# The first projection of a two-block transformer kernel: operands split before the squares, and the gates' arithmetic moved back

## What is computed

```python
def _layer(x, norm_w, w_in, qk_gain_q, qk_gain_k, rpb, conv_w, a_log, dt_bias, dn_norm_w, w_out):
    h = _rmsnorm(x, norm_w)                       # x * rsqrt(mean(x*x) + EPS) * norm_w
    proj = jnp.einsum('bld,de->ble', h, w_in)
    aq, ak, av, az, dq, dk, dv, dz, b_f, a_f, b_b, a_b = _split_proj(proj)
    aq = _rmsnorm(heads(aq, NA_HEADS), qk_gain_q)
    ak = _rmsnorm(heads(ak, NA_HEADS), qk_gain_k)
    attn = _neighbourhood_attention(aq, ak, heads(av, NA_HEADS), rpb) * jax.nn.silu(az)
    qkv = jax.nn.silu(_centred_depthwise_conv(jnp.concatenate([dq, dk, dv], axis=-1), conv_w))
    dq, dk, dv = jnp.split(qkv, 3, axis=-1)
    dq, dk, dv = _l2norm(to_bhld(dq)), _l2norm(to_bhld(dk)), to_bhld(dv)
    # gates: beta = sigmoid(b), g = -exp(a_log) * softplus(a + dt_bias)
    ...
    return x + y
```

## Time and profile before

| | |
|---|---|
| median of 3 runs | 2832.3 us (2832.14 to 2832.37) |
| the profiled execution | 2832.62 us, span of the core 2830.8 us |
| mean granted TensorE clock | 0.977 of full |
| PE busy | 2679.3 us, 95% of the span |
| PEld / DVE / ACT / POOL busy | 76% / 41% / 38% / 44% |
| span 0 to 10 us | PE busy 0.00 us |
| span 10 to 20 / 20 to 30 / 30 to 40 us | PE busy 3.24 / 4.87 / 7.36 us |
| span 40 to 50 us | PE busy 10.00 us |
| first projection, PE's matmuls | 16.1 us to 434.2 us of the span |

### The profile page before, as it was taken

The page is one execution under the profiler, slowest core; times in us unless marked ns, Lnnn a source line. Parts: engine busy times, 40 slices in busy tenths (PEclk is TensorE's granted clock), DMA queues, the critical chain, the costliest instruction groups (busy, mean ns, idle before and its releaser), DMA issues.

```text
span 2830.8 us, 33041 instructions
## 1 busy us (share of the span) xinstructions
PE 2679.3 (95%) x13337; PEld 2150.5 (76%) x13337; DVE 1174.1 (41%) x1631; ACT 1072.3 (38%) x1593; POOL 1243.0 (44%) x717
## 2 busy tenths in 40 slices
PE   6999998988969999999999999899999999999997
PEld 4778875667858888887888777666788888788885
DVE  6465666655663222222222327667532222222223
ACT  4443445634544422233322333656443222232222
POOL 2222222554026555556555554311455454565554
PEclk8999998989989999999999999999999999999998
DMA  3222415441143222223222232100222222323331
GB/s 132 90 88 96 150 45 203 135 142 52 38 145 115 97 97 97 97 97 104 97 97 97 98 130 91 40 8 1 99 95 98 97 97 97 112 90 108 116 103 69
DMA packets 93880, 273.20 MB, mean 97 GB/s; under 512 B 25944, under 2 KB 26136, under 8 KB 93600
## 3 DMA queue, kind: packets, MB, share of 16 engines
q1 hardware_dynamic: 93728, 271.09, 28.2%
HBM read 240.05 MB, written 31.00 MB: 96 GB/s over the span
## 4 chain that ended last, share of the span: by engine, by line
PE 82%; DVE 6%; POOL 5%; ACT 3%; DMA 2%; issue 1%; SPq 1%; POOLq 0%; DVEq 0%; ACTq 0%
PE ps L350 23%; PE ps L351 23%; PE ps L352 23%; PE ps L875 2%; ACT t L366 2%; PE ps L895 2%; PE ps L859 2%; POOL t L1336 1%; POOL t L1333 1%; PE ps L491 1%; DVE t L1009 1%; PE ps L1437 1%; POOL t L1834 1%; POOL t L415 1%; ACT t L958 1%
## 5 line engine op out<-in xcount | busy, mean ns | idle before, releaser
L366 ACT ACTIVATE t<-t 128x1024 fp32r<-128x1024 f32 (+5 forms) x961 | 735.3, 810 | 1392.1 <-PE ps L352 650.6
L415 POOL TENSOR_TENSOR t<-t 128x1024 fp32r<-128x1024 f32 x356 | 862.5, 2427 | 874.7 <-ACT t L366 874.6
L350 PE MATMUL ps<-t 128*128 128x512 f32 (+1 forms) x3034 | 1199.0, 395 | 47.5 <-DVE t L528 18.4
L352 PE MATMUL ps<-t 128*128 128x512 f32 (+1 forms) x3034 | 1181.4, 389 | 0.0
L351 PE MATMUL ps<-t 128*128 128x512 f32 (+1 forms) x3034 | 1181.3, 389 | 0.0
L350 PEld LDWEIGHTS ps<-t 128*128 128x128 f32 x3034 | 572.0, 189 | 184.8 <-issue 53.0
L351 PEld LDWEIGHTS ps<-t 128*128 128x128 f32 x3034 | 572.5, 189 | 120.7 <-issue 6.5
L352 PEld LDWEIGHTS ps<-t 128*128 128x128 f32 x3034 | 571.9, 188 | 118.5
L2050 DVE SCALAR_TENSOR_TENSOR t<-ps,t 128x512 f32<-128x512 f32 x192 | 132.7, 691 | 315.0 <-PE ps L352 277.2
L2106 POOL TENSOR_TENSOR t<-t 128x512 fp32r<-128x512 f32 x84 | 108.7, 1295 | 332.4 <-ACT t L366 332.4
L2027 DVE TENSOR_TENSOR t<-ps,t 128x512 f32<-128x512 f32 x84 | 58.1, 692 | 396.2 <-PE ps L352 396.2
(11 more groups left out here) (167 smaller groups left out, 1884.6 us busy)
## 6 DMA issues: line engine op xcount, KB each, us to landing
t<-in_wts_dram SPq DMA_DIRECT2D x356, 512.0 KB, 3.5
t<-pj SPq DMA_DIRECT2D x39, 512.0 KB, 5.9
pj<-t SPq DMA_DIRECT2D x32, 512.0 KB, 2.7
t<-in_rpb_dram SPq DMA_DIRECT2D x8, 736.0 KB, 7.7
t<-in_xT_dram SPq DMA_DIRECT2D x8, 512.0 KB, 10.5
t<-grow_d SPq DMA_DIRECT2D x8, 512.0 KB, 8.4
t<-beta_d SPq DMA_DIRECT2D x8, 512.0 KB, 9.5
t<-in_xT_dram SPq DMA_DIRECT2D x16, 256.0 KB, 4.0
```

Of the source, the lines that this page charges most:

```text
L350: e.matmul(out, ah, bh, start=start, stop=False)
L352: return e.matmul(out, al, bh, start=False, stop=stop)
L366: return e.activation(out, in_, fn, scale=scale)
L415: e.tensor_tensor(lo[:], T.raw[n % NR][:], hi[:].bitcast(F), SUB).then_inc(*w_lo.up(n))
```

## The change

- **Operands first.** ACT makes H of all eight chunks, then splits weights 1 and 2, then makes the eight squares; before, H and square alternated, behind the weights 0 to 2. DVE makes all eight Lo, then adds all seven squares; POOL adds none. The squares now take turns in t1 and t3.
- **x first.** SP issues weights 0, then the eight chunks of x, then weights 1 to 5.
- **Tile 0 by chunks.** PE runs both halves of chunk k before chunk k + 1. The sum for the factor is behind tile 1 instead of in the middle of tile 0.
- **Order of tiles.** The first eight behind the gates are silu, dv, dq, norm, norm, v, dk, silu; before they were dq, silu, dk, v, dv, norm, norm, silu.
- **Gates later.** `gates_1` stands behind y of tile 1; the gates' transpose is in PE's step 4 (was 2) ahead of half two, cum in step 5 (was 3), rows in step 6 (was 4).
- **Table.** ACT loads the table for Exp and Ln as its first instruction.

```diff
-for _c, _rows in enumerate([(16, 12, 20, 8, 24, 0, 4, 28), (24, 16, 0, 4, 8, 20, 12, 28), ...
+for _c, _rows in enumerate([(12, 24, 16, 0, 4, 8, 20, 28), (24, 16, 0, 4, 8, 20, 12, 28), ...
...
+    square_at = lambda k: (I_.t2, I_.t1, I_.t3)[0 if k == 0 else 1 + k % 2]
...
     def pe_inproj(e, w):
...
-                m = pe_half(e, w, n, slot(n % 3)[:, halves[0]], 0, I_.H, I_.Lo, ready)
-            if n == 0:
-                buf, before = aside.take("x", [(p_var, "x")])
-                factor(buf, before)
+                if n == 0:
+                    hi, lo = weights_of(n)
+                    w.wait_ge(w_lo, n)
+                    for k in range(KC):
+                        for s, key in ready(k):
+                            w.wait_ge(s, key)
+                        for h in halves:
+                            m = mm3(e, slot(n)[:, h], (hi[:, tok[k]], lo[:, tok[k]]),
+                                    (I_.H[:, k, h], I_.Lo[:, k, h]), k == 0, k == KC - 1)
+                    m.then_inc(*w_used.up(n))
+                else:
+                    pe_half(e, w, n, slot(n % 3)[:, halves[0]], 0, I_.H, I_.Lo, ready)
...
-            if n < N_INPROJ:
-                pe_half(e, w, n, slot(n % 3)[:, halves[1]], 1, I_.H, I_.Lo, ready).then_inc(*w_used.up(n))
-            if n == 2:
+            if n == 4:
                 w.wait_ge(p_gd, "beta")
                 w.wait_ge(p_gd, "g")
                 turn(0, I_.ev[0][0:64, 2:L + 2], 64)
-            if n == 3:
+            if 0 < n < N_INPROJ:
+                pe_half(e, w, n, slot(n % 3)[:, halves[1]], 1, I_.H, I_.Lo, ready).then_inc(*w_used.up(n))
+            if n == 1:
+                buf, before = aside.take("x", [(p_var, "x")])
+                factor(buf, before)
+            if n == 5:
                 buf, before = aside.take("cum", [(p_gd, "ed")])
...
-            if n == 4:
+            if n == 6:
                 buf, before = aside.take("rows", [(p_gd, "rows")])
...
     def dve_inproj(e, w):
...
-            if k % 2:
-                w.wait_ge(p_sq, k)
-                w.wait_ge(*((p_sq, 0) if k == 1 else (acc_by(k - 1), k - 1)))
-                e.tensor_tensor(I_.t2[:], I_.t2[:], I_.t1[:], ADD).then_inc(*acc_by(k).up(k))
+        for k in range(1, KC):
+            w.wait_ge(p_sq, k)
+            if k > 1:
+                w.wait_ge(p_acc, k - 1)
+            e.tensor_tensor(I_.t2[:], I_.t2[:], square_at(k)[:], ADD).then_inc(*p_acc.up(k))
...
-                if m == 0:
+                if m == 1:
                     gates_1()
...
     def act_inproj(e, w):
-        for n in range(3):
-            act_weights(e, w, n)
+        act_weights(e, w, 0)
         for k in range(KC):
             w.wait_ge(x_in[k], k)
             act(e, I_.H[:, k, :], X[:, k, :], ACT.Copy, scale=NH("norm1", k)).then_inc(*p_hi.up(k))
-            if k == 0:
-                act(e, I_.t2[:], X[:, k, :], ACT.Square).then_inc(*p_sq.up(k))
-            else:
-                if k > 1:
-                    w.wait_ge(acc_by(k - 1), k - 1)
-                act(e, I_.t1[:], X[:, k, :], ACT.Square).then_inc(*p_sq.up(k))
+        act_weights(e, w, 1)
+        act_weights(e, w, 2)
+        for k in range(KC):
+            if k > 2:
+                w.wait_ge(p_acc, k - 2)
+            act(e, square_at(k)[:], X[:, k, :], ACT.Square).then_inc(*p_sq.up(k))
...
     def sp_inproj(e, w):
+        sp_weights(e, w, 0)
         for k in range(KC):
-            if k < NR:
-                sp_weights(e, w, k)
             e.dma_start(X[:, k, :], A["xT"][k]).then_inc(*x_in[k].up(k))
-        for n in range(NR, 6):
+        for n in range(1, 6):
             sp_weights(e, w, n)
...
     def act_all(e, w):
+        table[0] = "lnexp"
+        e.preload_act_table_set("natural_log_exp_and_others")
         w.wait_ge(scaled, 0)
```

More of the change, by code:

```diff
@@ L20 @@
 IN_ORDER = [32]
-for _c, _rows in enumerate([(16, 12, 20, 8, 24, 0, 4, 28), (24, 16, 0, 4, 8, 20, 12, 28), (24, 16, 0, 4, 8, 20, 12, 28),
+for _c, _rows in enumerate([(12, 24, 16, 0, 4, 8, 20, 28), (24, 16, 0, 4, 8, 20, 12, 28), (24, 16, 0, 4, 8, 20, 12, 28),
                             (24, 16, 0, 4, 20, 28, 8, 12)]):
@@ L449, in build @@
     p_sum, p_turn, p_gate = kinds("p_pe", 3)
-    p_lo, p_acc_d, p_edge, p_y, p_conv, p_var, p_var2, p_norm0, p_norm, p_gd = kinds("p_dve", 10)
+    p_lo, p_acc, p_edge, p_y, p_conv, p_var, p_var2, p_norm0, p_norm, p_gd = kinds("p_dve", 10)
     p_hi, p_sq, p_silu, p_square, p_ln, p_rs, p_rs2, p_tk, p_ga = kinds("p_act", 9)
-    p_acc = [p_acc_d, sig("p_acc_p")]
     aside = ring([slot(3)])
     y_of = lambda n: I_.ev[n % 4][:, 2:L + 2]
-    acc_by = lambda k: p_acc[1 - k % 2]
+    square_at = lambda k: (I_.t2, I_.t1, I_.t3)[0 if k == 0 else 1 + k % 2]
     def pe_inproj(e, w):
         def factor(buf, before):
-            w.wait_ge(acc_by(KC - 1), KC - 1)
+            w.wait_ge(p_acc, KC - 1)
             for h in halves:
@@ L630, in dve_inproj @@
                 variance(n - 2)
-            if n == 2:
+            if n == 3:
                 gates_2()
-            if n == 4:
+            if n == 6:
                 w.wait_ge(p_ga, "eg")
@@ L729, in pool_inproj @@
             pool_weights(e, w, n)
[L730 to L733, removed]
         for n in range(3, N_INPROJ):
@@ L764, in sp_inproj @@
                 e.dma_start(kt_d[IN_ORDER[m] - 20], I_.tk[:]).then_inc(*store_tk.up(m))
-            if n == 1:
+            if n == 2:
                 w.wait_ge(p_gd, "beta")
                 e.dma_start(beta_d[:], I_.ev[0][0:8, 2:L + 2]).then_inc(*row_store[0].up(0))
-            if n == 4:
+            if n == 6:
                 w.wait_ge(p_gd, "rows")
```

## The result

The changed kernel takes 2815.16 us (median of four runs, 2814.34 to 2815.68) where the kernel before takes 2832.34 (median of four, 2832.14 to 2836.03): 0.9934 of it, 95% interval 0.992 to 0.9949. The forecast was 2815.6 in a range of 2810 to 2822. The profiled execution is 2815.0 us with a span of 2813.2, 17.6 us shorter than the span of before.

A forecast was written before the change was run, and what follows sets the result against it. PE bounds the kernel (82% of the last chain), its start paced by operands waiting on additions of squares. Gains and losses, 20.9 - 3.2 - 1.7 - 0.7 + 1.4 = 16.7 us, give 2815.6 us, range 2810 to 2822.

The forecast's parts named there:

- Tile 0: Projection's start: PE begins at 10.2 us, runs 3.5 us at half rate (bound 5.0), ends the tile at 22.7 us.
- gain so far: Projection's start: tile 2 begins at 35.35 instead of 56.22 us, gaining 20.9 us (18.5 with all bounds against it).
- Additions: Under tile 1: DVE's seven additions of squares end at 32.5 us, with 1.1 us to spare, covering 8.7 us.
- The new wait: In tile 5, PE waits 3.2 us before summing tile 3, until ACT has copied tile 2's transpose.
- three holds by POOL: Behind the factor: POOL delays a scalar_tensor_tensor, the gates' tensor_tensor and tile 3's convolution on DVE, 5.9 us in all.
- The clock behind it: After PE's wait in tile 5, a lower granted clock costs 1.7 us more (0 to 2.5).
- Tile 6: After half one of tile 6, PE waits 0.7 us (0 to 2) for the gates' copies on DVE.
- Waits that go: In the projection, PE's old waits of 1.2 us for two transposes in one step and 0.2 us vanish, gaining 1.4.
- A: Projection: no new PE wait, POOL's splits miss DVE's SBUF work; gain 20 to 22.3 us, 2810.0 to 2812.5; chance 0.20.
- B: Projection: longer chain, PE's wait 5 us, more clock loss, smaller start gain; gain 10.4 us, down to 2822; chance 0.12.
- C: Behind the projection: a later stage is bound by something not tied to it; no change, 2832 us; chance 0.03.
- D: Tiles 0 to 2: TensorE stays at half rate, 10.9 us a tile; slower, 2848 us with three more tiles; chance 0.03.

The follow-up runs named there:

- e8: Changed kernel, but PE sums the squares behind tile 0 instead of behind tile 1; 2822.21 us in one execution.
- e1: Changed kernel, but ACT's copy of tile 2's transpose stands ahead of tile 3's Silu and Square; 2815.03 us in one execution.
- e6: Changed kernel, but squares and their additions again alternate with the operands on ACT and DVE; 2822.73 us in one execution.
- e3: Changed kernel, but ACT copies weights 4 and 5 behind its gates' arithmetic, so POOL splits them beside DVE's reciprocal; 2812.29 us in one execution.
- e7: Changed kernel, but tile 0 runs half one over all chunks, then half two, as before; 2818.00 us in one execution.
- e4: Changed kernel without the table load as ACT's first instruction; 2817.48 us in one execution.
- e2: Changed kernel with tiles 3 and 4 exchanged (silu, dv, norm, dq); 2814.07 us in one execution, median 2811.42 when timed again.
- b2: Changed kernel with the edits of e1, e2 and e3, plus three unread matmuls of constants ahead of tile 0; median 2808.70 us.

## Why the prediction was right, point by point

- **Loads and operands.** x7 was to land at 16.5 us; its issue at 5.6 us and landing 10.6 later make 16.2. PE's first matmul was to come at 10.2 and came at 10.43. POOL's hold of Lo0 is there: it takes 1.84 us and ends 1.1 behind the split.
- **Tile 0.** 4.4 us at half rate against the 3.5 taken and the 5.0 kept as a bound: 0.5 us too good. The sum ended at 36.4 instead of 35.35. The second matmul of tile 2 starts at 56.45 us before and at 36.43 after, so the term "gain so far" is 20.0 us, not 20.9.
- **Additions.** They end at 32.4 us (32.5 said), under tile 1; e8 shows what this cover is worth.
- **The new wait.** Foreseen from 75.3 to 78.5, measured from 76.3 to 79.16: 2.88 us against 3.2, ended by the instruction named. Of the three holds by POOL the first is 3.30 us long, the third makes four steps take 7.25 instead of 5.25, and L578 is 2.30 us long. The prediction's working had 2.4 for it (54.7 to 57.1); the 3.3 in its list of signs does not follow from that working.
- **The clock behind it.** 1.70 us (e1 against the changed kernel), as said; the granted clock is 0.59 over 79.2 to 83.2 us. That it fits to a tenth is luck, since e6 lost 2.9 us behind the same gap.
- **Tile 6.** 0.7 us said, none measured. From the end of the sum of tile 3 to the end of DVE's copies for the gates it is 12.2 us in the changed kernel, in e1, e3 and e7 alike. PE's own work between is 11.6 us at full rate, hence the waits of 0.6 to 0.7 us in those three; in the changed kernel the lower clock stretched it to 12.3 us. So 0.6 of the 1.70 us of the clock would have been waited anyway: two terms that the prediction added cover one another in part.
- **Waits that go.** The 1.2 us ahead of two transposes in one step and the 0.2 at 98 us are gone.
- **Sum.** 20.0 - 2.9 - 1.7 + 1.4 = 16.8 us, and the mark says 16.7, where I had 20.9 - 3.2 - 1.7 - 0.7 + 1.4 = 16.7. The start was over-priced by 0.9 us, the waits behind it by 1.0; that the total agrees to 0.5 us is partly luck.
- **Behind the projection** I expected no change. The spans say 0.9 us more gain, from terms that happen to oppose: the gain grows from 16.7 us at the mark to 18.1 in the attention's first tiles (49.0 and 47.6) and to 19.1 at the rows below, falls to 16.7 in the last stretch of the kernel, and is 17.6 at the end. PE behind the same wait near the end, before and after:

```profile
2795.81 0.50 PE L2003 MATMUL ps<-t 128*128 128x512 f32 x1 [2.32 <-DVE t L2040]
```

```profile
2776.76 0.80 PE L2008 MATMUL ps<-t 128*128 128x512 f32 x1 [2.32 <-DVE t L2045]
```

From there to PE's next wait it is 20.1 us before and 22.4 after, at mean granted clocks of 0.98 and 0.85. In e4, e6 and e7 the same matmul takes 0.49 us, as in the kernel before, so this fall comes with the execution and not with the change. I had no term for it, and the range had room for it only because of other bounds.

Of the rivals, A (no wait) is what e2 makes true, and the marks of its two executions give 22.4 and 21.6 us against before where A said 20 to 22.3. B, C and D did not happen. The half of D that is true, that a start at half rate costs, is worth 1.3 to 1.7 us (b2).

## What to carry to other kernels

When an edit makes the bounding engine arrive earlier, write down who else has to be earlier too: here DVE's chain from the factor over the gates to two convolutions was hidden by PE's slow start, and 4.6 of the 20.0 us won at the start came back as one wait and its clock loss. A wait of the kind is cheapest to remove by order alone (e2 exchanges two tiles). And compare executions at a mark in the middle of the trace as well as by total time, since a fall of TensorE's clock elsewhere can be as large as the effect.

## What the runs showed of the hardware

- The same kernel's TensorE clock does not fall at the same places in each execution: 12 us at a mean granted clock of 0.60 in one and 0.86 in the other, 2.4 us of time. Behind a gap of 2.32 us a matmul took 0.50 us in one kernel and 0.80 in another; behind 2.06 us the full rate was kept (four matmuls in 1.96 us), behind 2.88 it was not (3.04 us), and behind 2.89 the same four took 3.40, 3.54 and 3.78 us in three kernels.
- At the very start (10.5 to 14.5 us of the changed kernel) the granted clock in the rows is 1.00 while the matmuls' starts are 0.43 us apart, against 0.23 at full rate. For the first microseconds the durations are to be believed, not the clock.
- A reciprocal on VectorE and a split on GpSimd run side by side without either being longer; a scalar_tensor_tensor of two SBUF operands ends 1.09 us behind the split (44.30 and 43.21 us). A tensor_scalar of one SBUF operand is held too (2.58 us instead of 0.75 in e3), and y, which reads one operand in PSUM and one in SBUF, is not (1.22 us at 116.35 beside a split from 115.91 to 118.71 in the changed kernel).
